# Grouped channel sums in the LayerNorm of a Conformer convolution, with more taps on TensorE

## What is computed

```python
a, gate = jnp.split(h @ w_in, 2, axis=-1)
u = a * jax.nn.sigmoid(gate)
u, tail = causal_depthwise_conv(u, buf, w_dw, b_dw)   # width 31, per channel
u = layernorm(u, ln_g, ln_b)                          # mean and variance over 1024 channels
return jax.nn.silu(u) @ w_out, tail
```

## Time and profile before

| what | value |
|---|---|
| median of 3 runs | 1505.46 us (1504.95 to 1506.41) |
| the profiled execution | 1503.89 us, span from first to last instruction 1502.3 us |
| granted TensorE clock | 1.000 |
| TensorE, VectorE, ScalarE, GpSimd busy | 97%, 65%, 61%, 18% of the span |

### The profile page before, as it was taken

One profiled execution on the slowest core, in us unless ns is written; L12 is line 12 of the kernel. 1 busy time (PEld: TensorE's weight loads), 2 busy tenths in 40 slices (PEclk: granted clock), 3 DMA queues, 4 the chain that ended last, 5 costly groups with the idle time before them and its releaser, 6 DMA issues.

```text
span 1502.3 us, 28454 instructions
## 1 busy us (share of the span) xinstructions
PE 1462.2 (97%) x11288; PEld 1347.5 (90%) x11288; DVE 978.2 (65%) x1473; ACT 909.3 (61%) x1658; POOL 266.1 (18%) x458
## 2 busy tenths in 40 slices
PE   5999999999999999999999989999999999999998
PEld 4787669999999999999889956679999999999997
DVE  4799966878744878645536346664887754777643
ACT  4699877777633776535425556664767643666633
POOL 2489810000000332100000022210000000322200
PEclk9999999999999999999999999999999999999999
DMA  9887683345554545554346366653255554454653
GB/s 378 309 299 271 255 283 120 99 160 170 183 174 142 162 162 167 192 166 128 125 136 236 113 225 225 225 197 117 76 178 168 169 185 153 142 169 168 196 165 102
DMA packets 72197, 273.76 MB, mean 182 GB/s; under 512 B 8080, under 2 KB 10144, under 8 KB 71680
## 3 DMA queue, kind: packets, MB, share of 16 engines
q1 hardware_dynamic: 65824, 247.69, 48.7%
q0 software_dynamic: 5952, 23.90, 4.8%
q10 hardware_dynamic: 288, 0.35, 0.1%
HBM read 262.80 MB, written 8.85 MB: 181 GB/s over the span
## 4 chain that ended last, share of the span: by engine, by line
PE 81%; DVE 10%; ACT 4%; issue 2%; DMA 2%; DVEq 0%; SPq 0%; ACTq 0%
PE ps L731 65%; DVE ps L1851 4%; PE ps L981 4%; PE ps L708 2%; PE ps L1034 1%; PE ps L1040 1%; PE ps L1017 1%; DMA ada_w<-w_ada_dram 1%; PE ps L1101 1%; PE ps L1068 1%; PE ps L1053 1%; PE ps L787 1%; DVE w_lo L1682 1%; DVE y L1968 1%; PE ps L897 1%
## 5 line engine op out<-in xcount | busy, mean ns | idle before, releaser
L731 PE MATMUL ps<-h_hi,w_hi 128*128 128x288 f32 x1920 | 570.6, 297 | 3.8 <-DVE w_lo L1682 2.1
L731 PE MATMUL ps<-h_lo,w_hi 128*128 128x288 f32 x1920 | 565.4, 294 | 0.0
L731 PE MATMUL ps<-h_hi,w_lo 128*128 128x288 f32 x1920 | 565.4, 294 | 0.0
L1682 DVE TENSOR_TENSOR w_lo<-raw,w_hi 128x1024 fp32r<-128x1024 f32 (+1 forms) x296 | 387.4, 1310 | 231.9 <-ACT w_hi L1245 231.4
L1245 ACT ACTIVATE w_hi<-raw 128x1024 fp32r<-128x1024 f32 (+1 forms) x309 | 346.9, 1124 | 108.3 <-PE ps L731 73.1
L731 PEld LDWEIGHTS ps<-h_hi,w_hi 128*128 128x128 f32 x1920 | 360.1, 188 | 10.3 <-DVE h_lo L1756 4.3
L731 PEld LDWEIGHTS ps<-h_lo,w_hi 128*128 128x128 f32 x1920 | 360.1, 188 | 0.9
L731 PEld LDWEIGHTS ps<-h_hi,w_lo 128*128 128x128 f32 x1920 | 360.1, 188 | 0.0
L731 PE MATMUL ps<-act_hi,w_hi 128*128 128x288 f32 x704 | 208.3, 296 | 0.0
L731 PE MATMUL ps<-act_lo,w_hi 128*128 128x288 f32 x704 | 207.7, 295 | 0.0
L731 PE MATMUL ps<-act_hi,w_lo 128*128 128x288 f32 x704 | 207.0, 294 | 0.0
(11 more groups left out here) (255 smaller groups left out, 2041.5 us busy)
## 6 DMA issues: line engine op xcount, KB each, us to landing
raw<-w_k_dram SPq DMA_DIRECT2D x245, 512.0 KB, 3.5
raw<-w_down_dram SPq DMA_DIRECT2D x64, 704.0 KB, 4.1
ada_w<-w_ada_dram SPq DMA_DIRECT2D x71, 512.0 KB, 6.1
k_page<-cache_kt_dram SPq DMA_DIRECT2D x32, 512.0 KB, 5.4
v_page<-cache_v_dram POOLq DMA_DIRECT2D x32, 512.0 KB, 5.3
ada_h<-w_ada_dram SPq DMA_DIRECT2D x7, 512.0 KB, 6.2
ada_u<-w_ada_dram SPq DMA_DIRECT2D x6, 512.0 KB, 15.1
ada_g<-w_ada_dram SPq DMA_DIRECT2D x6, 512.0 KB, 5.9
```

Source lines behind the costliest of these rows:

```text
L731: mm = pe.matmul(ps[:, BANK[b], 0:HALF], lhsT=w[s][:, kb * P:(kb + 1) * P], rhs=v[:, at, :] if down else v[:, at, lo:hi], start=(at == 0 a ...
L1682: dve.tensor_tensor(w_lo[s][:, 0:cols], raw[n % RING][:, 0:cols], w_hi[s][:, 0:cols].bitcast(F32), ALU.subtract).then_inc(s_lo, 1)
```

## The change

Four edits.

1. `PE_TAPS` of chunk 7 goes from 15 to 18, and VectorE's share of it falls from 10 to 7. ScalarE makes three more diagonals.
2. The mean sums of chunks 0 to 5 (`MEAN_GROUPED` = 6) become `mean_groups(h)`: matmuls with 32-column weights of 1/32 (`sum_w`), each to one of four column groups of the array, chunk n to group n mod 4. Each group's 32 partitions then hold the same partial sum. ScalarE copies that from PSUM to `mean_part`, and `mean_total(h)` adds the four with one matmul by `mean_w`, ahead of the ordinary mean sums of chunks 6 and 7. TensorE does the groups between tap 10 and tap 11 of chunk 7 and the totals behind the seven `ada_h` pieces.
3. The sums of squares go the same way: `square_sum` puts the two chunks of a pair in two column groups; after the last pair ScalarE copies to `sq_part`, TensorE adds by `square_total(h)`, and `ln_scale(h)` on ScalarE waits for that. `square_total(0)` stands ahead of the mean sum of chunk 7, half 1; `square_total(1)` stands behind the two ring pieces of kb = 7.
4. For chunk 6, `seq_conv` comes five VectorE steps sooner, ahead of the last five tap steps.

```diff
-PE_TAPS = [0] * (C - 1) + [15]
+PE_TAPS = [0] * (C - 1) + [18]
@@ TensorE
+            def mean_groups(h):
+                pe.wait_ge(pair_free[h], C)
+                for n in range(MEAN_GROUPED):
+                    pe.wait_ge(conv_summed, n + 1)
+                    if h:
+                        pe.wait_ge(conv_seq, n + 1)
+                    t = n % 4
+                    mm = pe.matmul(ps[32 * t:32 * t + 32, MEAN_BANK[h], 0:HALF], lhsT=sum_w[:],
+                                   rhs=y[:, n, h * HALF:(h + 1) * HALF], start=(n < 4), stop=(n + 4 >= MEAN_GROUPED),
+                                   skip_group_check=True)
+                mm.then_inc(mean_grouped, 1)
+
+            def mean_total(h):
+                pe.wait_ge(mean_copied, h + 1)
+                pe.matmul(ps[:, MEAN_BANK[h], 0:HALF], lhsT=mean_w[:], rhs=mean_part[:, h, :], start=True, stop=False)
@@ square_sum(h, p)
-                    mm = pe.matmul(ps[:, 2 * STAT + h, 0:HALF], lhsT=mean_w[:], rhs=pair[:, j, :],
-                                   start=(p + j == 0), stop=(p == C // 2 - 1 and j == 1))
+                    t = (2 * p + j) % 4
+                    mm = pe.matmul(ps[32 * t:32 * t + 32, 2 * STAT + h, 0:HALF], lhsT=sum_w[:], rhs=pair[:, j, :],
+                                   start=(p < 2), stop=(p >= 2), skip_group_check=True)
                 mm.then_inc(sq_used, 1)
+            def square_total(h):
+                pe.wait_ge(sq_copied, h + 1)
+                pe.matmul(ps[:, 2 * STAT + h, 0:HALF], lhsT=mean_w[:], rhs=sq_part[:], start=True, stop=True)\
+                    .then_inc(sq_total, 1)
@@
             late_pieces(ADA_RING)
-            conv_taps(C - 1)
+            conv_taps(C - 1, range(0, DIAG_TILE))
+            pe.wait_ge(sum_w_made, 1)
+            for h in range(2):
+                mean_groups(h)
+            conv_taps(C - 1, range(DIAG_TILE, PE_TAPS[-1]))
             late_pieces(len(OWN_TILE))
-            for n in range(C - 1):
+            for h in range(2):
+                mean_total(h)
+            for n in range(MEAN_GROUPED, C - 1):
                 mean_sum(n, 0)
                 mean_sum(n, 1)
             mean_sum(C - 1, 0)
             late_pieces(ADA_RING)
             for p in range(C // 2):
                 square_sum(0, p)
+            square_total(0)
             mean_sum(C - 1, 1)
             late_pieces(len(OWN_AGAIN))
@@ behind the three blocks together (kb = 0 to 7)
+            square_total(1)
@@ ScalarE, between the taps of chunk 6 and those of chunk 7
+            for h in range(2):
+                act.wait_ge(pair_free[1], C)
+                act.wait_ge(mean_grouped, h + 1)
+                act.activation(mean_part[:, h, :], ps[:, MEAN_BANK[h], 0:HALF], ACT.Copy).then_inc(mean_copied, 1)
@@ ln_scale(h)
                 act.wait_ge(sq_used, (h + 1) * (C // 2))
+                act.activation(sq_part[:], ps[:, 2 * STAT + h, 0:HALF], ACT.Copy).then_inc(sq_copied, 1)
+                act.wait_ge(sq_total, h + 1)
                 act.activation(rs[:, lo:hi], ps[:, 2 * STAT + h, 0:HALF], ACT.Ln, bias=eps_col[:, 0:1]).then_inc(a_ln, 1)
@@ VectorE
-                late_taps(i - 1, range(early, made))
+                first = made if i < C - 1 else made - 5
+                late_taps(i - 1, range(early, first))
                 seq_conv(i - 1)
+                late_taps(i - 1, range(first, made))
```

More of the change, by code:

```diff
@@ L85 @@
 LATE_SUM = 5
+MEAN_GROUPED = C - 2
 PE_SUMS = [sum(n > 0 for n in PE_TAPS[:i + 1]) for i in range(C)]
@@ L437, in trunk_kernel @@
         sig = place("sig", [P, TT], at=(at := temp(shared)))
-        odd_taps = place("odd_taps", [P, TP], at=at)
+        sq_part = place("sq_part", [P, HALF], at=[at[0], at[0] + TP * 4])
+        at[0] += TP * 4
         mod_t = place("mod_t", [P, 4 * P], at=at)
@@ L443, in trunk_kernel @@
         x_first = place("x_first", [P, TT], at=temp(shared))
+        mean_part = place("mean_part", [P, 2, HALF], at=temp(shared))
         g_pad = [place(f"g_pad{j}", [P, WF - 1 + HALF], at=(at if j else (at := temp(shared)))) for j in range(2)]
@@ L482, in trunk_kernel @@
         o_seq = place("o_seq", [P, 2 * P], at=behind_raw(1))
+        sum_w = place("sum_w", [P, 32], at=behind_raw(2))
         q_seq = place("q_seq", [P, PAIRS, 4 * TS], at=behind_raw(2))
@@ L543, in trunk_kernel @@
         a_ln = sem("ln_logarithm")
+        sum_w_made, mean_grouped, mean_copied = sem("sum_weights_made"), sem("mean_groups_done"), sem("mean_groups_copied")
+        sq_copied, sq_total = sem("sq_groups_copied"), sem("sq_groups_summed")
         ysq_ready, y_acc = sem("y_squared"), sem("y_sq_added")
@@ L800, in turn_group, with conv_taps @@
                 mm.then_inc(mod_turned, 1)
-            def conv_taps(i):
+            def conv_taps(i, part):
                 pe.wait_ge(pair_free[1], i + 1)
-                for k in range(PE_TAPS[i]):
+                for k in part:
                     pe.wait_ge(diag_made, k + 1)
@@ L809, in conv_taps @@
                                    start=(k == 0), stop=(k == PE_TAPS[i] - 1))
-                mm.then_inc(taps_pe, 1)
+                if part.stop == PE_TAPS[i]:
+                    mm.then_inc(taps_pe, 1)
             def first_pieces(q):
@@ L865, in _ @@
                     turn_group(GROUP_END[b])
+            def mean_groups(h):
[12 more added lines that the diff above has]
+                pe.matmul(ps[:, MEAN_BANK[h], 0:HALF], lhsT=mean_w[:], rhs=mean_part[:, h, :], start=True, stop=False)
             def mean_sum(n, h):
-                if n == 0:
-                    pe.wait_ge(pair_free[h], C)
                 if n < C - 1:
@@ L878, in mean_sum @@
                 mm = pe.matmul(ps[:, MEAN_BANK[h], 0:HALF], lhsT=mean_w[:], rhs=y[:, n, h * HALF:(h + 1) * HALF],
-                               start=(n == 0), stop=(n == C - 1))
+                               start=False, stop=(n == C - 1))
                 if n == C - 1:
@@ L2223, in _ @@
             pool.memset(four_diag[:], 1.0).then_inc(s_const, 1)
+            pool.memset(sum_w[:], 1.0 / 32).then_inc(sum_w_made, 1)
             pool.wait_ge(s_const, 9)
```

## The result

The changed kernel takes **1513.84 us** (median of 6 runs, 1513.27 to 1515.64) against 1505.39 us (1504.03 to 1506.41) for the kernel before on the same chip: ratio 1.0056, 95% interval 1.0046 to 1.0066. It is 8.45 us slower. I forecast 3.5 us slower, with a range to 1512.0: the side was right, the size was not, and the time lies outside the range.

What follows compares the result with a forecast made beforehand. TensorE was taken to bound the stage. Terms: +1.1 us at the first ring pieces, -0.45 for three pairs of squares, +2.86 at the blocks' end, +3.5 in all: 1509.0 us, range 1504.0 to 1512.0.

Steps and rivals of the forecast that it cites:

- The projection would start 1.4 sooner: Output projection's start: faster mean sums and squares of half 0 would move it from 204.67 to 203.3 us.
- A grouped pair: Squares of half 1 in the output projection: each pair costs 0.82 us with group switching, saving 0.15, 0.6 in all.
- the 2.86 of the sum: End of the three blocks: ScalarE's ln waits for the new total, delaying weight 19 and TensorE by 2.86 us.
- the second ring load: Ring pieces of kb = 1: this load lands at 209.2 us, so its use starts 1.1 us later than before.
- ten more of 0.524 MB at 418 GB/s take 12.5: Loads behind the first ada_g load, landed at 191.9: transfer time in us up to the second ring load, excluding the store's share.
- hardly moves the start of the projection: Last ada_g piece, at 203 or so: little effect on the projection's start, hidden by the stall behind it.
- rival C: TensorE's clock falls after stalls of 2.4 and 2.8 us; one block at half clock adds 3.2: 1512.2 us, chance 0.05.
- The half-1 term: Squares of half 1: 2.86 us lost waiting for the total, less 0.45 saved on three pairs.
- Rivals A: Late loads arrive in time because the store moves or shares without cost: +0.9, 1506.3 us, chance 0.22.
- B: Loads in time and a grouped pair costs only 0.5 us: 1505.0, or 1502.2 with the total's wait hidden; chance 0.10.
- D: Grouped sums do not run at once on TensorE: +7 us, 1512 to 1516, chance 0.03.
- early enough for what follows: ScalarE's products of chunk 7 end about 1 us sooner, in time for later work.

Runs made afterwards that it cites:

- e2: The changed kernel with the convolution-state stores issued earlier, right after the sum for chunk 5: 1507.82 us, +2.42 against the kernel before.
- e5: The changed kernel with early stores and half 1's squares at full width again, without copy, total or wait: 1504.31 us, -1.41 against the kernel before.
- e11: The changed kernel run once more, unaltered, for a second trace: 1513.41 us, +7.97 against the kernel before.
- e9: The changed kernel, stores still late, with half 1's squares at full width again: 1509.90 us, +4.46 against the kernel before.
- after: The changed kernel itself, with all four edits: 1513.84 us, +8.45 against the kernel before.
- e3: The changed kernel with square_total(1) ahead of the last two ring pieces instead of behind them: 1511.07 us, +5.67 against the kernel before.
- e4: The changed kernel with the seven ada_h pieces ahead of the mean's groups and the last taps: 1511.43 us, +6.03 against the kernel before.
- e8: The changed kernel with early stores and chunk 6's seq_conv back behind the last five tap steps: 1508.45 us, +2.73 against the kernel before.
- e12: The changed kernel with early stores and five useless matmuls in TensorE's idle time ahead of block 19: 1506.19 us, +0.60 against the kernel before.
- e10: The changed kernel with early stores, half 1's squares at full width and 15 taps instead of 18: 1506.38 us, +0.94 against the kernel before.

## Where the prediction was right and where it was wrong

**Right, with sizes.** The groups of the mean take 179.46 - 177.40 = 2.06 us (I took 2.2). The first `ada_g` load is issued at 188.5 and lands at 191.9, both as forecast. VectorE waits 0.74 us ahead of `seq_conv(6)` (0.7). The projection would start 1.4 sooner: 1.47 in e2, and in e5 203.06 - 168.23 = 34.83, 1.44. A grouped pair with the nine instructions behind it takes 0.61 + 1.38 = 1.99 in the chain above, a full one 0.97 + 1.18 = 2.15: 0.16 saved, where I had 0.15. From the end of the three blocks to block 19 I had 5.97 us; it is 5.71 + 0.26 = 5.97 in e11, and the loss is the 2.86 of the sum. Block 19 itself starts at 231.08, outside the 226 to 230 that I had named. The Trainium skill's rule that a change of tiling mode drains TensorE (TensorEngine Tiling (Array Packing), Key Properties) held in its direction: without such a price e2 would have shown 1.9 us less in the blocks, and it shows 0.70. The traces give the price, not what takes it.

**Wrong, first: when the loads arrive.** I had the second ring load at 209.2; it landed at 212.2. Its part in the result was to be 2.5 us (1.4 of gain lost, and 1.1); e2 and e5 put it at 6.0 and 5.9. The step that failed is "ten more of 0.524 MB at 418 GB/s take 12.5", to which I added nothing but the store's share. The stretches of e11 (columns as above), then its queues in 196 to 203 and in 191.9 to 212.2 (packets, MB, share of 16 engines):

```profile
190.00:192.00 2.00, 2.00 (x10) 1.44 (x8) 1.93 (x4) 2.00 (x10) 2.00 (x4) 1.00 1.00 393
192.00:196.00 4.00, 3.79 (x28) 1.03 (x27) 3.66 (x10) 3.68 (x7) 0.50 (x3) 1.00 0.89 300
196.00:203.00 7.00, 5.15 (x28) 1.50 (x28) 6.76 (x10) 5.23 (x10) 0.00 (x0) 1.00 1.01 320
203.00:211.00 8.00, 5.81 (x34) 2.90 (x33) 4.24 (x11) 4.94 (x12) 0.00 (x0) 1.00 1.03 413
```

```profile
q0 software_dynamic: 188, 1.35, 57.9%
q1 hardware_dynamic: 240, 0.89, 43.3%
...
q1 hardware_dynamic: 1611, 5.85, 78.6%
```

The store itself cost what I said. In 196 to 203 the loads moved 0.89 MB, which take 2.1 us at 418 GB/s; 4.9 of the 7 us were lost, and I had 4.8. Two things stood in no term. From 192 to 196, when the stores are issued (190.4 and 191.2) but hardly a packet of them moves, only 1.2 MB come (300 GB/s), 1.1 us less than at 418. And until the second ring load landed, 5.85 MB had been loaded, not 10 x 0.524 = 5.24: the third and fourth ring loads were under way beside it and took 0.61 MB, 1.5 us. 191.9 + 12.5 + 4.9 + 1.1 + 1.5 = 211.9, against 212.2. My upper bound of 211 was not high enough either. The slow stretch could have been read from the kernel before, which has it as well behind its issues of the store (330 GB/s in 192 to 195). In e11 the landing is 2.8 us later, behind the first tap, than forecast; the medians ask for 3.5. The trace of e9 has all of it: its second ring load is used 44.42 us behind the first tap (213.55 - 169.13), where I had 40.9 (209.3 - 168.4), and nothing in that stretch runs at the lower clock. So the landing alone, which differs by 0.8 us between these two traces, can make the 3.5. In other executions the waits for `ada_g` are followed by the lower clock too, as in the first profile of after and in e3 (granted clock 0.5 from 204.8 on, behind an idle time of 2.37); what that adds to the medians no run isolates.

I also had the place of the wait wrong. I expected it in front of the ring pieces of kb = 1 (about 2.4 us) and wrote that the last `ada_g` piece "hardly moves the start of the projection". In e11 TensorE waits 2.84 us for `ada_g` and 0.92 (0.69 and 0.23) for the ring, and the projection starts 1.94 later, not at its old time.

**Wrong, second: the clock, rival C.** I gave it 0.05 because no row of the stage showed the lower level. The idle time of 3.15 comes with it in each trace of a kernel that has it unfilled (after, e2, e4, e8, e11); e3, with 1.95, and e12, with the idle time filled, run block 19 at the full clock. Its cost is 1.56 us in e11 and 2.43 in e2 by the traces, 1.6 in the medians of e12 against e2 (at the edge of what medians tell). I had sized it at 3.2, a whole block at half speed. The half-1 term was to be 2.86 - 0.45 = 2.4; it is 3.9, and the clock is what is missing.

Together: 3.5 too little for the loads and 1.5 for the clock are the 5.0 between 3.5 and 8.45. Rivals A and B are out since the loads were late, and D since the groups took 2.06.

**A judgement that fell.** I had written that ScalarE's products of chunk 7 come "early enough for what follows", with the sooner `seq_conv(6)` as a matter of VectorE's time. The trace of e8 shows that ScalarE needs it: 1.11 us of TensorE's wait for the first squares go by it.

## What to carry to other kernels

A sum over narrow column groups saves little when it stands alone between full-width matmuls (0.16 us of the 0.97 that a pair takes at full width), and its second step puts a wait into an in-order engine: ask what is queued behind that wait before counting the turns saved. When TensorE's work moves, ask which loads it releases and what then shares the DMA engines with them: a store that cost nothing moved 6 us, and one moved issue took it off again. An idle time of TensorE can have two prices, its length and the clock behind it: here those of 2.3 us and more had both, those up to 1.95 only the first. Filling it with useless matmuls measures the second.

## What the runs showed of the hardware that was not expected

**The store and the loads share by packets, not by bytes.** The queues of e11 in 197 to 202 (packets, MB, share of 16 engines):

```profile
q0 software_dynamic: 121, 1.07, 66.2%
q1 hardware_dynamic: 114, 0.42, 35.6%
```

Both queues moved nearly the same number of packets, 121 and 114, but the store 1.07 MB and the loads 0.42. In e9 it is 117 and 112 in the same stretch, in e2, around its earlier store, 112 and 116 in 183 to 188; in the kernel before it is 122 and 67 in 197 to 202, but there the loads had run dry and moved 0.04 MB until 201. By the Trainium skill (DMA: Bandwidth & Descriptors, Queues, rings and completion order) each DMA engine alternates between the queues that have work, a packet at a time; the near-equal counts agree, if the profile counts the same packets. So while it lasts, a store with larger packets leaves the loads much less than half: 0.42 of 1.49 MB here.

**Loads were slower just ahead of such a store:** 300 GB/s in 192 to 196 in e11, 330 in 192 to 195 in the kernel before, against 418, between its issue on GpSimd and its first packets. What takes that time was not tried.

**The lower clock came around the end of an idle time of 2.3 to 3.2 us.** In this stage the granted clock went to 0.5 (1.2 instead of 2.4 GHz) around the end of an idle time of 2.34 (e10), 2.37 (e3), 2.57 and 2.79 (after) and 3.15 us (after, e2, e4, e8, e11), and cost 1.6 to 2.4 us of the matmuls behind the last of these. It can fall before TensorE begins again (e2: granted clock 0.70 in 225 to 226, block 19 at 226.81) or after (e11: 0.73 in 232 to 233, block 19 at 231.08). The longest idle time in this stage without it was 1.95 (e3). In the input stage, where TensorE waits between short pieces of work, it comes and goes from run to run of one kernel: the first trace of after has it there, the second has not.
